# Gate and up products of a two-part fp32r matmul: one 512-column product takes the x parts side by side, their halves are added on the way out

## The chip, the cores and the metric

The kernel runs on one core of a Trainium2 chip. The metric is the device time of one execution in microseconds (us). TensorE (PE) multiplies, with weight loads on a row of their own (PEld); VectorE (DVE) and ScalarE (ACT) work beside it; GpSimd (POOL) has almost nothing to do; SyncE (SP) issues the DMAs.

## The reference

Two layers of: half-step SwiGLU, a hybrid mixer (sliding-window attention beside gated linear attention), half-step SwiGLU; 256 tokens, width 1024, feed-forward width 2816, all in float32. The change touches the feed-forward blocks, of which there are four:

```python
def swiglu(x, w_gate, w_up, w_down):
    a = jnp.einsum('bsd,df->bsf', x, w_gate)
    u = jnp.einsum('bsd,df->bsf', x, w_up)
    return jnp.einsum('bsf,fd->bsd', jax.nn.silu(a) * u, w_down)

for l in range(2):
    x = x + 0.5 * swiglu(rmsnorm(x, ffn1_norm[l]), ffn1_w_gate[l], ffn1_w_up[l], ffn1_w_down[l])
    x = x + hybrid_mixer(rmsnorm(x, mix_norm[l]), ...)
    x = x + 0.5 * swiglu(rmsnorm(x, ffn2_norm[l]), ffn2_w_gate[l], ffn2_w_up[l], ffn2_w_down[l])
```

## The kernel before

**Two-part arithmetic.** Each fp32 operand is split into a rounded fp32r part and the fp32r rest: weights into `whi` and `wlo`, activations into `xhi` and `xlo` (or `h_parts` for the hidden values). A product is then three matmuls into the same place in PSUM: whi with xhi, whi with xlo, wlo with xhi (`three`, lines 356 to 358). Tokens are the moving operand: 256 columns; the stationary operand is a 128x128 block of weights, loaded anew for each of the three.

**Units.** The weights come in units of 256 columns of gate or up weights (or 256 rows of down weights), 1 MB each, in three slots that go round: `raw` is filled by a DMA, ACT rounds it into `whi` (`split_hi`, line 791), DVE subtracts for `wlo` (`split_lo`, line 1021), and then PE may start. A gate or up unit has two tiles of 128 hidden features (`FT` = 2) and eight blocks of the contraction (`KT` = 8), so 16 triples; a down unit too. `unit_done` counts finished units; ACT waits on it before it overwrites a slot.

**A feed-forward block** has 11 groups of 256 hidden features. PE's order is: gate and up of group 0 (banks 2 and 7, at the end of the stage before), gate and up of group 1, down of group 0, and in a loop gate of g, up of g, down of g-1; at the end down of group 10 (`finish`). Gate products of groups 1 to 10 go to PSUM bank 0, up products to bank 1. DVE multiplies them on their way out by `rB`, the row of 1/rms values (`gate_out`, line 1103; `up_out`, line 1108), ACT takes the silu (line 816), DVE multiplies both (line 1111), ACT and DVE split the result (lines 823 and 1115), and `hlo_done` lets the down unit of that group go. Down products accumulate in banks 4 to 7.

**The norm's detour.** The 1/rms values are spread over the partitions by TensorE into bank 3 (`spread_r`, line 413), in the midst of or just after the gate unit of group 1, and DVE copies them to `rB` (`norm_b`, line 1095; semaphore `rb_done`). Group 0's gate values wait in bank 2 for that, and `a_done` counts gate values that have left.

Of the kernel before, what the change touches and what calls it, by code (L numbers as in the profile page):

```python
# [22 lines left out]
F32 = mybir.dt.float32  # L23
F32R = mybir.dt.float32r
I32 = mybir.dt.int32
ALU = mybir.AluOpType
# [69 lines left out]
def trunk(nc, xt, par_d, gain0_d, cst_d, fg, fu, fd, w_in, w_out, out):  # L96
    ctx = ExitStack()
    with ctx:
# [12 lines left out]
        xhi = sb("xhi", [P, KT, SEQ], F32R)  # L111
        xlo = sb("xlo", [P, KT, SEQ], F32R)
# [51 lines left out]
        sg = sb("sg", [P, 4, SEQ])  # L164
        at32 = work[:, 0:4, :]
# [6 lines left out]
        ps = [ctx.enter_context(nc.psum_tensor(f"ps{i}", [P, 512], F32)) for i in range(8)]  # L172
# [47 lines left out]
        rb_done = sem("rb_done")  # L220
        a_done, silu_done, u_done, h_done, hhi_done, hlo_done = (
# [132 lines left out]
        def _(pe):  # L354
# [19 lines left out]
            def up(slot, turn, bank):  # L374
                split_ready(slot, turn)
                for ft in range(FT):
                    last = up_tile(tiles(bank)[:, ft, :], slot, ft)
                last.then_inc(unit_done, 1)
# [58 lines left out]
            def first_pieces(u, bank):  # L437

                for p in range(PIECES):
                    if p < PIECES - 1:  # L440
                        pe.wait_ge(lo_piece, (PIECES - 1) * u + p + 1)
                    else:
                        split_ready(u, 0)
                    for ft in range(FT):
                        for k in (2 * p, 2 * p + 1):
                            w_hi, w_lo = weights(u, k, UC, ft * P, P)
# [53 lines left out]
            def ffn(f, l):  # L500
# [284 lines left out]
        def _(act):  # L785
# [27 lines left out]

            def silu(n):
# [10 lines left out]
            def ffn(f, l, after):  # L825
# [20 lines left out]
                split_hi(2, t + g)  # L846
                silu(grp + g)
                h_hi(1, grp + g)
# [167 lines left out]
        def _(dve):  # L1016
# [83 lines left out]
            def gate_out(n, unit, bank=0):  # L1100

                dve.wait_ge(unit_done, ST + unit + 1)
                nc.vector.tensor_tensor(a32[:, :, :], tiles(bank), r_tiles(2), ALU.mult).then_inc(a_done, 1)  # L1103

            def up_out(n, unit, bank=1):

                dve.wait_ge(unit_done, ST + unit + 1)
                nc.vector.tensor_tensor(u32[:, :, :], tiles(bank), r_tiles(2), ALU.mult).then_inc(u_done, 1)  # L1108
# [9 lines left out]
            def ffn(f, l, v, after):  # L1118
# [6 lines left out]
                gate_out(grp, 3 * t, 2)  # L1125
                up_out(grp, 3 * t + 1, 7)
                split_lo(1, t + 1)
                h_lo(0, grp)
                with dve.Fori(1, GROUPS - 1) as g:

                    split_lo(2, t + g)
                    gate_out(grp + g, 3 * (t + g) - 1)

                    split_lo(0, t + g + 1)
                    up_out(grp + g, 3 * (t + g))
# [5 lines left out]
                gate_out(grp + g, 3 * (t + g) - 1)  # L1141
                up_out(grp + g, 3 * (t + g))
# [328 lines left out]
```

## Time and profile before

| | |
|---|---|
| median of 3 runs | 964.71 us (963.52 to 965.16) |
| the profiled execution | 965.2 us, its span from first to last instruction 963.2 us |
| PE matmul, PE weight load | 950.4 us (99%), 942.7 us (98%) of the span |
| DVE, ACT | 613.3 us (64%), 456.5 us (47%) |
| mean granted TensorE clock | 0.993 |
| mean HBM traffic | 176 GB/s |

A busy PE is not a PE at its peak: matmuls are pipelined, so that a row's length (some 0.28 us) is more than twice the step from one row's start to the next. The steps are what counts, and they are read from the start times.

### The profile page before, as it was taken

To read this page: it belongs to the slowest core of one execution; us is meant where nothing else is said; L and a number is where in the kernel's file an instruction comes from. 1 tells how busy PE (TensorE), PEld (TensorE's weight loads), DVE (VectorE), ACT (ScalarE), POOL (GpSimd) and SP (SyncE) were. 2 spreads that over 40 slices of the span, in tenths; PEclk is the share of its full clock that TensorE was granted. 3 is DMA by queue.
4 is the path that set the end of the run, shared out by engine and by line. 5 is a ranking of instruction groups with operands and counts; after the bars stand their busy time and mean duration, and the time that the engine had idled before them with its cause. 6 is when DMAs were issued, how large, how long until landed. Compare 5 with 4: busy or idle time off the path is not lost.

```text
span 963.2 us, 19406 instructions
## 1 busy us (share of the span) xinstructions
PE 950.4 (99%) x8188; PEld 942.7 (98%) x8188; DVE 613.3 (64%) x732; ACT 456.5 (47%) x490; POOL 2.8 (0%) x6
## 2 busy tenths in 40 slices
PE   8999999999999999999999999999999999999996
PEld 8999999999999999999999999999999999999996
DVE  6756555587758665555686555557786785555653
ACT  6433443457645433443554344346584634334332
POOL 0000000000000000000000000000000000000001
PEclk9999999999999999999999999999999999999997
DMA  8665565553246665555556555555522665656621
GB/s 284 216 216 176 184 203 180 178 179 118 77 153 200 210 202 175 185 195 187 174 191 209 174 186 194 186 177 167 183 66 70 216 220 189 203 174 190 201 87 44
DMA packets 130613, 169.05 MB, mean 176 GB/s; under 512 B 3216, under 2 KB 116112, under 8 KB 130576
## 3 DMA queue, kind: packets, MB, share of 16 engines
q1 hardware_dynamic: 130576, 168.52, 54.4%
q8 instruction: 28, 0.46, 0.2%
q14 instruction: 9, 0.07, 0.0%
HBM read 167.46 MB, written 1.05 MB: 175 GB/s over the span
## 4 chain that ended last, share of the span: by engine, by line
PE 93%; DVE 3%; ACT 2%; DMA 1%; issue 0%; SPq 0%; POOL 0%; DVEq 0%
PE ps L356 29%; PE ps L357 29%; PE ps L358 29%; PE ps L413 1%; PE ps L563 1%; DMA raw<-in_ffn_w_gate 1%; PE ps L576 1%; DVE resid L1048 0%; DVE wlo L1021 0%; PE ps L722 0%; ACT sq L812 0%; ACT whi L791 0%; PE ps L700 0%; DVE work L1291 0%; DVE xlo L1026 0%
## 5 line engine op out<-in xcount | busy, mean ns | idle before, releaser
L1021 DVE TENSOR_TENSOR wlo<-raw,whi 128x2048 fp32r<-128x2048 f32 (+1 forms) x159 | 355.9, 2239 | 252.9 <-ACT whi L791 252.9
L356 PE MATMUL ps<-xhi,whi 128*128 128x256 f32 x1680 | 471.9, 281 | 0.0
L357 PE MATMUL ps<-xlo,whi 128*128 128x256 f32 x1680 | 470.7, 280 | 0.0
L358 PE MATMUL ps<-xhi,wlo 128*128 128x256 f32 x1680 | 469.3, 279 | 0.0
L791 ACT ACTIVATE whi<-raw 128x2048 fp32r<-128x2048 f32 (+1 forms) x159 | 297.3, 1870 | 166.1 <-PE ps L358 160.1
L356 PEld LDWEIGHTS ps<-xhi,whi 128*128 128x128 f32 x1680 | 316.2, 188 | 1.7 <-issue 1.0
L357 PEld LDWEIGHTS ps<-xlo,whi 128*128 128x128 f32 x1680 | 315.9, 188 | 0.0
L358 PEld LDWEIGHTS ps<-xhi,wlo 128*128 128x128 f32 x1680 | 315.0, 187 | 0.0
L356 PE MATMUL ps<-h_parts,whi 128*128 128x256 f32 x768 | 212.7, 277 | 0.0
L357 PE MATMUL ps<-h_parts,whi 128*128 128x256 f32 x768 | 212.4, 277 | 0.0
L358 PE MATMUL ps<-h_parts,wlo 128*128 128x256 f32 x768 | 212.3, 276 | 0.0
L356 PEld LDWEIGHTS ps<-h_parts,whi 128*128 128x128 f32 x768 | 144.4, 188 | 0.1
L358 PEld LDWEIGHTS ps<-h_parts,wlo 128*128 128x128 f32 x768 | 144.4, 188 | 0.0
L357 PEld LDWEIGHTS ps<-h_parts,whi 128*128 128x128 f32 x768 | 144.4, 188 | 0.0
L823 ACT ACTIVATE h_parts<-work 128x512 fp32r<-128x512 f32 x44 | 27.8, 633 | 145.0 <-DVE work L1111 145.0
L816 ACT ACTIVATE work<-work 128x512 f32<-128x512 f32 x44 | 27.8, 632 | 131.9 <-DVE work L1103 131.9
L1115 DVE TENSOR_TENSOR h_parts<-work,h_parts 128x512 fp32r<-128x512 f32 x44 | 30.5, 692 | 30.8 <-ACT h_parts L823 30.8
L1108 DVE TENSOR_TENSOR work<-ps,rB 128x512 f32<-128x512 f32 x44 | 30.1, 684 | 3.0 <-PE ps L358 3.0
L1111 DVE TENSOR_TENSOR work<-work 128x512 f32<-128x512 f32 x44 | 30.5, 693 | 2.1 <-ACT work L816 0.7
L1103 DVE TENSOR_TENSOR work<-ps,rB 128x512 f32<-128x512 f32 x44 | 30.2, 686 | 0.1
L1048 DVE SCALAR_TENSOR_TENSOR resid<-ps,resid 128x512 f32<-128x512 f32 x24 | 16.6, 690 | 11.2 <-PE ps L358 11.2
L805 ACT ACTIVATE xhi<-resid,par 128x256 fp32r<-128x256 f32 x40 | 18.2, 503 | 7.7 <-DVE resid L1048 7.3
(150 smaller groups left out, 485.5 us busy)
## 6 DMA issues: line engine op xcount, KB each, us to landing
raw<-in_ffn_w_down SPq DMA_DIRECT2D x44, 1024.0 KB, 4.9
raw<-in_ffn_w_up SPq DMA_DIRECT2D x43, 1024.0 KB, 5.3
raw<-in_ffn_w_gate SPq DMA_DIRECT2D x42, 1024.0 KB, 5.4
raw<-in_w_in SPq DMA_DIRECT2D x12, 1024.0 KB, 5.2
raw<-in_w_in SPq DMA_DIRECT2D x8, 512.0 KB, 4.6
raw<-in_w_out SPq DMA_DIRECT2D x8, 512.0 KB, 4.4
raw<-in_w_in SPq DMA_DIRECT2D x2, 1088.0 KB, 5.2
raw<-in_ffn_w_gate SPq DMA_DIRECT2D x8, 256.0 KB, 7.1
```

The costliest lines, as they stand in the source:

```text
L356: pe.matmul(o, w_hi, x_hi, start=start, stop=False, skip_group_check=True)
L357: pe.matmul(o, w_hi, x_lo, start=False, stop=False, skip_group_check=True)
L358: return pe.matmul(o, w_lo, x_hi, start=False, stop=stop, skip_group_check=True)
L791: nc.scalar.activation(h, r, ACT.Copy).then_inc(hi_done, 1)
L805: nc.scalar.activation(xhi[:, m, :], resid[:, m, :], ACT.Copy, scale=gain[:, m:m + 1]).then_inc(xhi_done, 1)
L816: nc.scalar.activation(s32[:, :, :], a32[:, :, :], ACT.Silu).then_inc(silu_done, 1)
L823: nc.scalar.activation(hhi[hb][:, :, :], h32[:, :, :], ACT.Copy).then_inc(hhi_done, 1)
L1021: nc.vector.tensor_tensor(lo, r, h.bitcast(F32), ALU.subtract).then_inc(lo_done, 1)
L1103: nc.vector.tensor_tensor(a32[:, :, :], tiles(bank), r_tiles(2), ALU.mult).then_inc(a_done, 1)
L1108: nc.vector.tensor_tensor(u32[:, :, :], tiles(bank), r_tiles(2), ALU.mult).then_inc(u_done, 1)
L1111: nc.vector.tensor_tensor(h32[:, :, :], s32[:, :, :], u32[:, :, :], ALU.mult).then_inc(h_done, 1)
L1115: nc.vector.tensor_tensor(hlo[hb][:, :, :], h32[:, :, :], hhi[hb][:, :, :].bitcast(F32), ALU.subtract).then_inc(hlo_done, 1)
```

## The change

`xhi` and `xlo` become two halves of one tensor `x_parts`, side by side for each contraction block, and the gate and up units of groups 1 to 10 of each feed-forward block use them as one moving operand of 512 columns: whi is loaded once for both, and the result goes to a whole bank, whi·xhi in its first half and whi·xlo in its second. The third product, wlo with xhi, has 256 columns and accumulates on the first half. A gate or up unit of two tiles so fills two banks, `gate_ps` (banks 0 and 1) and `up_ps` (banks 2 and 3). On the way out ACT copies the second halves to SBUF (`cross`, in the space of the mixer's `PT`), DVE adds the first halves to that, and a further DVE instruction multiplies by `rB`. Group 0, the down units and the mixer keep `three`. Since banks 2 and 3 hold group 0's gate values and the spread 1/rms values, PE waits for `rb_done` and `a_done` before the up unit of group 1.

```diff
-        xhi = sb("xhi", [P, KT, SEQ], F32R)
-        xlo = sb("xlo", [P, KT, SEQ], F32R)
+        x_parts = sb("x_parts", [P, KT, 2, SEQ], F32R)
+        xhi, xlo = x_parts[:, :, 0, :], x_parts[:, :, 1, :]
...
+        cross = PT[:, :, :].rearrange("p h c -> p (h c)")[:, 0:4 * SEQ].rearrange("p (u f t) -> p u f t", u=2, f=FT)
+
+        def wide_halves(wide):
+            parts = wide[:, :].rearrange("p (f a t) -> p f a t", f=FT, a=2)
+            return parts[:, :, 0, :], parts[:, :, 1, :]
...
-        ps = [ctx.enter_context(nc.psum_tensor(f"ps{i}", [P, 512], F32)) for i in range(8)]
+        gate_ps = ctx.enter_context(nc.psum_tensor("gate_ps", [P, 1024], F32))
+        up_ps = ctx.enter_context(nc.psum_tensor("up_ps", [P, 1024], F32))
+        ps = [w[:, 512 * i:512 * i + 512] for w in (gate_ps, up_ps) for i in range(2)]
+        ps += [ctx.enter_context(nc.psum_tensor(f"ps{i}", [P, 512], F32)) for i in range(4, 8)]
...
+            def wide_two(wide, slot, ft, k):
+
+                o = wide[:, 512 * ft:512 * ft + 512]
+                w_hi, w_lo = weights(slot, k, UC, ft * P, P)
+                pe.matmul(o, w_hi, x_parts[:, k, :, :].rearrange("p a t -> p (a t)"),
+                          start=k == 0, stop=False, skip_group_check=True)
+                return pe.matmul(o[:, 0:SEQ], w_lo, xhi[:, k, :], start=False, stop=k == KT - 1,
+                                 skip_group_check=True)
...
-                    up_tile(tiles(0)[:, 0, :], 2, 0)
+                    wide_tile(gate_ps, 2, 0)
                     spread_r(5 * l + 4 * f, rs_y)
-                    up_tile(tiles(0)[:, 1, :], 2, 1).then_inc(unit_done, 1)
-                up(0, t + 1, 1)
+                    wide_tile(gate_ps, 2, 1).then_inc(unit_done, 1)
+                pe.wait_ge(rb_done, v + 1)
+                pe.wait_ge(a_done, grp + 1)
+                up_wide(0, t + 1, up_ps)
                 pe.wait_ge(hlo_done, grp + 1)
...
                 with pe.Fori(2, GROUPS) as g:
                     pe.wait_ge(a_done, grp + g)
-                    up(2, t + g - 1, 0)
+                    up_wide(2, t + g - 1, gate_ps)
                     pe.wait_ge(u_done, grp + g)
-                    up(0, t + g, 1)
+                    up_wide(0, t + g, up_ps)
...
+            def cross_out(unit, u, wide):
+
+                act.wait_ge(unit_done, ST + unit + 1)
+                nc.scalar.copy(cross[:, u, :, :], wide_halves(wide)[1]).then_inc(cross_done, 1)
...
                 split_hi(2, t + g)
+                cross_out(3 * (t + g) - 1, 0, gate_ps)
                 silu(grp + g)
+                cross_out(3 * (t + g), 1, up_ps)
                 h_hi(1, grp + g)
...
+            def wide_out(i, u, wide, dst, done):
+
+                dve.wait_ge(cross_done, 2 * i + u + 1)
+                nc.vector.tensor_tensor(dst[:, :, :], cross[:, u, :, :], wide_halves(wide)[0], ALU.add
+                                        ).then_inc(wide_step, 1)
+                dve.wait_ge(wide_step, 2 * i + u + 1)
+                nc.vector.tensor_tensor(dst[:, :, :], dst[:, :, :], r_tiles(2), ALU.mult).then_inc(done, 1)
```

On PE, at the first up unit of the first feed-forward block (`L413` or `L438` is `spread_r`, what follows is the up unit of group 1), the order before is:

```order
L358 MATMUL ps<-xhi,wlo 128x256
L413 MATMUL ps<-cst,rs_y 128x128 [waits rs_step]
L413 MATMUL ps<-cst,rs_y 128x128
L356 MATMUL ps<-xhi,whi 128x256 [waits lo_done]
L357 MATMUL ps<-xlo,whi 128x256
L358 MATMUL ps<-xhi,wlo 128x256
```

and now:

```order
L390 MATMUL gate_ps<-x_parts,wlo 128x256
L438 MATMUL up_ps<-cst,rs_y 128x128 [waits rs_step]
L438 MATMUL up_ps<-cst,rs_y 128x128
L388 MATMUL up_ps<-x_parts,whi 128x512 [waits lo_done,a_done,rb_done]
L390 MATMUL up_ps<-x_parts,wlo 128x256
L388 MATMUL up_ps<-x_parts,whi 128x512
```

A triple has become a pair, and the up unit's first matmul waits for DVE twice more.

On ACT, the end of a feed-forward block (last gate and up group, after the loop; `L791` or `L821` is `split_hi`, `L816` or `L851` the silu, `L823` or `L858` is `h_hi`) before:

```order
L791 ACTIVATE whi<-raw 128x2048 [waits unit_done,loaded2]
L816 ACTIVATE work<-work 128x512 [waits a_done]
L823 ACTIVATE h_parts<-work 128x512 [waits h_done]
L791 ACTIVATE whi<-raw 128x2048 [waits unit_done,loaded0]
L791 ACTIVATE whi<-raw 128x2176 [waits unit_done,loaded1]
```

and now:

```order
L821 ACTIVATE whi<-raw 128x2048 [waits unit_done,loaded2]
L847 COPY PT<-gate_ps 128x512 [waits unit_done]
L851 ACTIVATE work<-work 128x512 [waits a_done]
L847 COPY PT<-up_ps 128x512 [waits unit_done]
L858 ACTIVATE h_parts<-work 128x512 [waits h_done]
L821 ACTIVATE whi<-raw 128x2048 [waits unit_done,loaded0]
```

Two copies out of PSUM have come in, the second one behind the silu.

On DVE, the same place (`L1021` or `L1060` is `split_lo`, `L1111` or `L1155` the product of silu and up, `L1115` or `L1159` is `h_lo`) before:

```order
L1021 TENSOR_TENSOR wlo<-raw,whi 128x2048 [waits hi_done]
L1103 TENSOR_TENSOR work<-ps,rB 128x512 [waits unit_done]
L1108 TENSOR_TENSOR work<-ps,rB 128x512 [waits unit_done]
L1111 TENSOR_TENSOR work<-work 128x512 [waits silu_done,u_done]
L1115 TENSOR_TENSOR h_parts<-work,h_parts 128x512 [waits hhi_done]
```

and now:

```order
L1060 TENSOR_TENSOR wlo<-raw,whi 128x2048 [waits hi_done]
L1147 TENSOR_TENSOR work<-PT,gate_ps 128x512 [waits cross_done]
L1150 TENSOR_TENSOR work<-work,rB 128x512 [waits wide_step]
L1147 TENSOR_TENSOR work<-PT,up_ps 128x512 [waits cross_done]
L1150 TENSOR_TENSOR work<-work,rB 128x512 [waits wide_step]
L1155 TENSOR_TENSOR work<-work 128x512 [waits silu_done,u_done]
L1159 TENSOR_TENSOR h_parts<-work,h_parts 128x512 [waits hhi_done]
```

Each value that leaves PSUM now takes two DVE instructions, and waits for ACT's copy instead of for PE.

## Rows read from the trace of the kernel before

**Rows 1.** The page: busy time, share of the span and instructions of each engine

```profile
PE 950.4 (99%) x8188; PEld 942.7 (98%) x8188; DVE 613.3 (64%) x732; ACT 456.5 (47%) x490; POOL 2.8 (0%) x6
```

**Rows 2.** The page: the chain that ended last, share of the span

```profile
PE 93%; DVE 3%; ACT 2%; DMA 1%; issue 0%; SPq 0%; POOL 0%; DVEq 0%
```

**Rows 3.** Timeline of PE, one loop turn: start us, length us, engine, line, operation

```profile
157.92 0.28 PE L356 MATMUL ps<-xhi,whi 128*128 128x256 f32 x1
...
169.23 0.28 PE L356 MATMUL ps<-h_parts,whi 128*128 128x256 f32 x1
...
174.68 0.28 PE L356 MATMUL ps<-xhi,whi 128*128 128x256 f32 x1
```

**Rows 4.** Timeline of PE, mixer of layer 1, where the clock is halved

```profile
738.28 0.42 PE L358 MATMUL ps<-xhi,wlo 128*128 128x256 f32 x1
...
740.42 0.41 PE L356 MATMUL ps<-h_parts,whi 128*128 128x256 f32 x1
```

**Rows 5.** Windows: busy us of PE, PEld, DVE, ACT, POOL; clock, DMA share, GB/s

```profile
738.30:740.30 2.00, 2.00 (x11) 2.00 (x11) 0.54 (x4) 0.00 (x0) 0.00 (x0) 0.50 0.00 0
157.90:169.20 11.30, 11.30 (x98) 11.30 (x97) 6.24 (x5) 4.90 (x4) 0.00 (x0) 1.00 0.57 188
```

**Rows 6.** Timeline of PE, mixer of layer 0: products with one moving column

```profile
266.12 1.92 PE L722 MATMUL ps<-ones,sq 128*128 128x1 f32 x16 [0.27 <-ACT sq L948]
```

**Rows 7.** Timeline of PE, mixer of layer 0: 272 moving columns, the widest there are

```profile
206.38 0.29 PE L356 MATMUL ps<-whi,xhi 128*128 128x272 f32 x1
...
208.90 0.29 PE L358 MATMUL ps<-whi,xlo 128*128 128x272 f32 x1
```

**Rows 8.** Timeline of PE and of DVE, group 1 of the first feed-forward block

```profile
28.99 0.60 PE L413 MATMUL ps<-cst,rs_y 128*128 128x128 f32 x4
29.35 0.36 PE L356 MATMUL ps<-xhi,whi 128*128 128x256 f32 x1
...
30.09 0.69 DVE L1103 TENSOR_TENSOR work<-ps,rB 128x512 f32<-128x512 f32 x1
```

**Rows 9.** Timeline of PE and of DVE, group 1 of the second block

```profile
312.75 0.28 PE L358 MATMUL ps<-xhi,wlo 128*128 128x256 f32 x1
...
310.69 0.69 DVE L1103 TENSOR_TENSOR work<-ps,rB 128x512 f32<-128x512 f32 x1
```

**Rows 10.** Groups of instructions by line and shape: busy us, mean ns, idle before

```profile
L946 ACT COPY work<-ps 128x512 f32<-128x512 f32 x4 | 2.3, 568 | 0.0
...
L1111 DVE TENSOR_TENSOR work<-work 128x512 f32<-128x512 f32 x44 | 30.5, 693 | 2.1 <-ACT work L816 0.7
L1103 DVE TENSOR_TENSOR work<-ps,rB 128x512 f32<-128x512 f32 x44 | 30.2, 686 | 0.1
```

**Rows 11.** Timelines of DVE, ACT and PE, last group of the first block

```profile
182.54 2.29 DVE L1021 TENSOR_TENSOR wlo<-raw,whi 128x2048 fp32r<-128x2048 f32 x1 [2.65 <-ACT whi L791]
184.75 0.68 DVE L1103 TENSOR_TENSOR work<-ps,rB 128x512 f32<-128x512 f32 x1
...
188.30 0.69 DVE L1115 TENSOR_TENSOR h_parts<-work,h_parts 128x512 fp32r<-128x512 f32 x1 [0.70 <-ACT h_parts L823]
...
185.47 0.63 ACT L816 ACTIVATE work<-work 128x512 f32<-128x512 f32 x1 [2.96 <-DVE work L1103]
187.63 0.63 ACT L823 ACTIVATE h_parts<-work 128x512 fp32r<-128x512 f32 x1 [1.54 <-DVE work L1111]
...
180.33 0.28 PE L356 MATMUL ps<-xhi,whi 128*128 128x256 f32 x1
...
185.98 0.28 PE L356 MATMUL ps<-h_parts,whi 128*128 128x256 f32 x1
...
191.43 0.28 PE L356 MATMUL ps<-h_parts,whi 128*128 128x256 f32 x1
```

**Rows 12.** Timelines of ACT and DVE in the loop turn of rows 3

```profile
163.78 1.91 ACT L791 ACTIVATE whi<-raw 128x2048 fp32r<-128x2048 f32 x1 [2.97 <-PE ps L358]
...
167.93 0.69 DVE L1103 TENSOR_TENSOR work<-ps,rB 128x512 f32<-128x512 f32 x1
```

More of the change, by code:

```diff
@@ L220, in trunk @@
         rb_done = sem("rb_done")
+        cross_done, wide_step = sem("cross_done"), sem("wide_step")
         a_done, silu_done, u_done, h_done, hhi_done, hlo_done = (
@@ L372, in up_tile, with wide_tile, up_wide @@
                 return last
-            def up(slot, turn, bank):
+            def wide_two(wide, slot, ft, k):
[5 more added lines that the diff above has]
+                                 skip_group_check=True)
+            def wide_tile(wide, slot, ft):
+                for k in range(KT):
+                    last = wide_two(wide, slot, ft, k)
+                return last
+            def up_wide(slot, turn, wide):
                 split_ready(slot, turn)
                 for ft in range(FT):
-                    last = up_tile(tiles(bank)[:, ft, :], slot, ft)
+                    last = wide_tile(wide, slot, ft)
                 last.then_inc(unit_done, 1)
@@ L445, in first_pieces @@
                         for k in (2 * p, 2 * p + 1):
+                            if u == 2:
+                                last = wide_two(gate_ps, u, ft, k)
+                                continue
                             w_hi, w_lo = weights(u, k, UC, ft * P, P)
@@ L846, in ffn @@
                 split_hi(2, t + g)
+                cross_out(3 * (t + g) - 1, 0, gate_ps)
                 silu(grp + g)
+                cross_out(3 * (t + g), 1, up_ps)
                 h_hi(1, grp + g)
@@ L1098, in r_tiles, with first_out, h_out @@
                 return rB[:, :].unsqueeze(1).to_broadcast([P, n, SEQ])
-            def gate_out(n, unit, bank=0):
+            def first_out(unit, bank, dst, done):
                 dve.wait_ge(unit_done, ST + unit + 1)
[L1103 to L1108, printed above, removed]
+                nc.vector.tensor_tensor(dst[:, :, :], tiles(bank), r_tiles(2), ALU.mult).then_inc(done, 1)
+            def wide_out(i, u, wide, dst, done):
[4 more added lines that the diff above has]
+                nc.vector.tensor_tensor(dst[:, :, :], dst[:, :, :], r_tiles(2), ALU.mult).then_inc(done, 1)
+            def h_out(n):
                 dve.wait_ge(u_done, n + 1)
@@ L1124, in ffn @@
                 dve.wait_ge(rb_done, v + 1)
-                gate_out(grp, 3 * t, 2)
-                up_out(grp, 3 * t + 1, 7)
+                first_out(3 * t, 2, a32, a_done)
+                first_out(3 * t + 1, 7, u32, u_done)
+                h_out(grp)
                 split_lo(1, t + 1)
                 h_lo(0, grp)
+                wide0 = (2 * l + f) * (GROUPS - 1) - 1
                 with dve.Fori(1, GROUPS - 1) as g:
                     split_lo(2, t + g)
-                    gate_out(grp + g, 3 * (t + g) - 1)
+                    wide_out(wide0 + g, 0, gate_ps, a32, a_done)
                     split_lo(0, t + g + 1)
-                    up_out(grp + g, 3 * (t + g))
+                    wide_out(wide0 + g, 1, up_ps, u32, u_done)
+                    h_out(grp + g)
                     h_lo(0, grp + g)
@@ L1140, in ffn @@
                 split_lo(2, t + g)
-                gate_out(grp + g, 3 * (t + g) - 1)
-                up_out(grp + g, 3 * (t + g))
+                wide_out(wide0 + g, 0, gate_ps, a32, a_done)
+                wide_out(wide0 + g, 1, up_ps, u32, u_done)
+                h_out(grp + g)
                 h_lo(1, grp + g)
```

## Prediction

> **What bounds the kernel now.** I read the page first: PE's matmul row is busy 99% of the span and its weight-load row 98%, while DVE has 64% and ACT 47% [rows 1]. The chain of work that ended last is PE for 93% of the span [rows 2]. So time is won or lost in how fast PE steps from one matmul to the next, and the other engines matter only where PE comes to wait for them. The timeline gives the step. In one loop turn the gate unit and the up unit take 96 matmuls from 157.92 to 169.23 us, and the down unit 48 matmuls from there to 174.68 [rows 3]: 11.31 / 96 = 117.8 ns and 5.45 / 48 = 113.5 ns each, in both cases 256 moving columns over a 128x128 block of weights. No gap is to be seen between units. A triple of the gate and up units is 3 x 117.8 = 353.4 ns.
>
> What is in a step of 117.8 ns? In layer 1's mixer there is a stretch with the clock granted at 0.50 [rows 5], which is 1.2 instead of 2.4 GHz, and there ten matmuls of 256 columns take 738.28 to 740.42 [rows 4], 214 ns each. Half of that, 107 ns, is the streaming of 256 columns at full clock. The full-clock step is 10.8 ns longer. A matmul with one moving column, whose streaming is nothing, steps at (1.92 - 0.25) / 15 = 111 ns [rows 6] (0.25 being what the last row's length adds, an estimate from the 0.28 of the other rows): that is what loading 128 columns of weights costs. So at 256 columns the stream (107) and the load beneath it (111) are nearly the same length, and the step lies a little above both. At half clock the stream of 214 ns hides the load wholly, and nothing is left over it.
>
> **The change, part by part.** It touches 4 blocks x 20 units (gate and up, groups 1 to 10) x 16 triples = 1280 triples. Each loses one matmul and one weight load, and becomes one matmul of 512 columns and one of 256.
>
> *The 512-column step.* No row has 512 columns. From below: 214 ns, the half-clock row, where a stream of equal length stands over a load of the same size. From above, by the widest row there is: 20 steps of 272 columns take 206.38 to 208.90 [rows 7], 126 ns each or 0.463 ns per column, and at that rate 512 columns take 237 ns. Between them lies a fixed extra of 10.8 ns, as 256 columns have it: 225 ns. I take 217, near the lower end, since the half-clock row is nearest in what matters: a load with twice its own time to hide in.
>
> *The 256-column step behind it.* Under it the load for the next wide product has to go, as now; I keep 117.8. The lower end is the load alone, 111.
>
> *Sum on PE.* 217 + 117.8 = 334.8 ns against 353.4: 18.6 ns less, times 1280 = 23.8 us less. The ends: 214 + 111 = 325 gives 36.4 us less; 225 + 117.8 = 342.8 gives 13.6 us less; 237 + 117.8 = 354.8 gives 1.8 us more.
>
> Here a rule speaks against the change. The row shows 117.8 ns where the stream is 107. By the Trainium skill ("TensorE: Matmul & The Clock Gate", section "Back-to-back issue gap"), a warm matmul's gap is its columns over 2.4 plus about 2.5 ns, so that a triple would be 327.5 now and 325 after: a saving of 2.5 ns per triple, 3.2 us in all, in place of my 23.8. The trace disagrees with the first of these figures by 26 ns per triple. The same section also gives a sustained 131 ns per pair of load and matmul at 512 columns. With it a pair would be 249 ns and the gain 134 us; no row here streams faster than 256 columns in 113.5 ns, which is 227 ns for 512.
>
> *The way out.* Per gate or up unit ACT gets a copy of 512 elements out of PSUM, 0.57 us, and DVE one more instruction of 0.69 [rows 10]: 80 x 0.57 = 46 us on ACT and 80 x 0.69 = 55 us on DVE. Both have room: in a gate and up stretch of 11.3 us DVE is busy 6.24 and ACT 4.90 [rows 5]. What counts is lateness. In the loop, gate values leave at 167.93 to 168.62 [rows 12]; now `a_done` comes some 0.75 later, and after it, in ACT's order, the silu, the next `split_hi`, the copy of the up halves. I follow it from the end of a gate unit, T = 157.92 + 48 x 0.1178 = 163.57, with the durations of these rows (`split_hi` 1.91, `split_lo` 2.29, the small steps 0.57 to 0.69 [rows 10, 11, 12]): the gate value begins to leave at T+4.4 and is done at T+5.8, silu T+6.5, `split_hi` T+8.4, copy T+9.0, `split_lo` T+10.7, up value T+12.1, h T+12.8, its two parts T+14.2, and the next `split_hi` and `split_lo` at T+17.7. PE wants h's parts and that slot at T+21.5 (an up, a down, a gate and an up unit later), and the next turn begins for ACT at T+16.2, when it is free. So nothing is late, and the work costs nothing while 3.8 us of cover remain.
>
> *The last group* has no such cover. PE starts its down unit (`finish`) straight after down of group 9, at 191.43, and the last part of h is ready at 188.30 + 0.69 = 188.99 [rows 11]. Now, from `split_lo`'s end at 184.75 on: add and multiply to 186.16, silu to 186.82, copy to 187.4, add and multiply to 188.83, product to 189.55, high part to 190.21, low part to 190.94. PE begins that group's up unit at 180.33 and so arrives at 180.33 + 16 x 0.3348 + 48 x 0.1135 = 191.14. A margin of 0.2 us where there were 2.4; if the pair is 325 ns, 0.04. I put 0.2 us for all four blocks together, and up to 1 us if an added step is 0.25 us longer than its row.
>
> *The new wait ahead of group 1's up unit.* In the first block PE spreads 1/rms at 28.99, begins the up unit at 29.35, and group 0's gate values leave bank 2 only at 30.09 + 0.69 = 30.78 [rows 8]. The wait stops PE for 30.78 - 29.35 plus some 0.1 to start again: 1.5 us. All later weights are queued behind it on PE, nothing else. In the three other blocks the spread is issued in the middle of the gate unit: the bank is free at 310.69 + 0.69 = 311.38, PE gets there at 312.75 [rows 9], or 0.15 sooner with faster pairs. No wait; the cover is 1.2 us.
>
> **Sum.** 965.2 (the profiled execution) - 23.8 + 1.5 + 0.2 = 943.1 us. The median before is 0.5 lower, 964.71, so 943 us, 2.3% less.
>
> **The rivals.**
>
> *The extra is a fixed price per matmul.* Then 225 + 117.8, and 965.2 - 13.6 + 1.7 - 0.5 = 952.8 us. For it: 272 columns also have more than their stream (126 against 114). Against it: the half-clock row, where the extra is nil. Chance 0.22.
>
> *The 256-column step gets shorter too*, towards the load's 111, because its own weights are ready long before: 325 ns, 965.2 - 36.4 + 1.7 - 0.5 = 930 us; half-way is 937. Chance of a step clearly shorter than I take, so that the time is below 936: 0.07.
>
> *The time goes with columns.* If the moving operand is read at 117.8 / 256 = 0.46 ns per column, 512 take 235.6, a pair is 353.4, nothing is saved, and the waits are left: 966 us. The fixed part alone could be small: 3 ns less per triple is 3.8 us, 962.6 us or, with the waits, about 963. The skill's formula, above, is of this kind. Measured, all these are no change. Chance 0.09. The 131 ns figure, by which the time would be about 831 us, gets 0.01.
>
> *Slower: a wide product steps at the rate of the 272-column row or worse.* 237 + 117.8 = 354.8 ns, 1.8 us more, and with the waits 965.2 + 1.8 + 1.7 - 0.5 = 968 us. From 256 to 272 columns the step grows by (126 - 117.8) / 16 = 0.5 ns per column, more than the stream's 0.42, which speaks for it; at 0.5 on all further columns 512 take 249 and the time is 984. Against it: the half-clock stretch has no such slope. It decides from 237 ns for 512 columns on. Chance 0.09.
>
> **How the numbers follow.** My forecast, roughly 936 to 948 us, has 0.52; the fixed price, 948 to 956, has 0.22; the shorter step 0.07; no gain 0.09; slower 0.09; the last 0.01 is far below all of them. Faster is the sum of the first three and the last. A measurement of this kernel tells some 0.2% (2 us) from no change. Faster 0.82, same 0.09, slower 0.09. The range 933 to 958 leaves out the two cases without a gain and the shortest times.
>
> **What would show it.** In the timeline of PE a loop turn's gate and up units: 32 pairs in about 10.7 us against 11.31, with starts 217 and 118 ns apart; down units unchanged at 5.45. In the waits of PE a new one of about 1.3 to 1.5 us at the first wide up unit, for DVE's work tile, and none at the three others. At each `finish` a gap under 0.1 us. DVE at some 668 us busy, ACT at 502. The prediction is wrong if the wide step is over 230 ns, if the last group's chain is longer than its rows say, or if the first wait is followed by a stretch at half clock, which would cost up to 1.7 us (3.4 us at half speed, as in layer 1's mixer).

## The result and the profile after

The changed kernel takes 971.56 us (median of 5 runs, 969.62 to 972.06) against 965.16 us of the kernel before beside it (5 runs, 963.52 to 967.22): a ratio of 1.0058, 95% interval 1.0041 to 1.0074. It is slower by 0.6%, and the forecast of 943 us was wrong in size and in sign. The profiled execution took 969.62 us, its span 967.7 us, at a mean clock of 0.996.

The page of the changed kernel, busy time of each engine and its costliest PE groups, answers to [rows 1]:

```profile
PE 954.3 (99%) x6908; PEld 888.4 (92%) x6908; DVE 668.2 (69%) x812; ACT 489.5 (51%) x570; POOL 2.8 (0%) x6
...
L388 PE MATMUL up_ps<-x_parts,whi 128*128 128x512 f32 x640 | 227.9, 396 | 1.3 <-DVE rB L1134 1.3
L388 PE MATMUL gate_ps<-x_parts,whi 128*128 128x512 f32 x640 | 228.0, 396 | 0.0
```

1280 matmuls and 1280 weight loads are gone (8188 to 6908), and PE is busy for 3.9 us longer. DVE has the forecast's 668 us. PE's matmul row says only that it never rests; the steps have to be read from start times, as before.

The timeline of PE, changed kernel, two loop turns (`L388` is the wide product, `L390` the one of wlo, `L366` the first of a down unit):

```profile
142.94 0.40 PE L388 MATMUL gate_ps<-x_parts,whi 128*128 128x512 f32 x1
143.18 0.28 PE L390 MATMUL gate_ps<-x_parts,wlo 128*128 128x256 f32 x1
...
154.26 0.28 PE L366 MATMUL ps<-h_parts,whi 128*128 128x256 f32 x1
...
159.91 0.39 PE L388 MATMUL gate_ps<-x_parts,whi 128*128 128x512 f32 x1
160.14 0.28 PE L390 MATMUL gate_ps<-x_parts,wlo 128*128 128x256 f32 x1
160.25 0.39 PE L388 MATMUL gate_ps<-x_parts,whi 128*128 128x512 f32 x1
160.48 0.28 PE L390 MATMUL gate_ps<-x_parts,wlo 128*128 128x256 f32 x1
160.60 0.40 PE L388 MATMUL gate_ps<-x_parts,whi 128*128 128x512 f32 x1
160.83 0.28 PE L390 MATMUL gate_ps<-x_parts,wlo 128*128 128x256 f32 x1
...
171.20 0.28 PE L366 MATMUL ps<-h_parts,whi 128*128 128x256 f32 x1
...
176.64 0.40 PE L388 MATMUL gate_ps<-x_parts,whi 128*128 128x512 f32 x1
```

Three things stand here. First, a wide step takes 0.23 us, then one of 0.12 follows; over all pairs of the loops the means are 233.4 and 119.7 ns, 353.1 together. The 32 pairs of a turn take 11.29 and 11.32 us by turns, where the 96 matmuls of [rows 3] took 11.31. **The pair costs what the triple cost.** Second, the down unit, which the change doesn't touch, takes 159.91 - 154.26 = 5.65 us in one turn and 176.64 - 171.20 = 5.44 us in the next: 117.7 and 113.3 ns per matmul. This alternates from turn to turn; only the last two down units of a block, which follow each other with no pair between them, are of the same kind. 21 of the 44 down units of the feed-forward blocks are of the slow kind, where before all 44 had 113.3. Third, the waits of PE:

```profile
PE up_ps L438 <- DVE rs_y L1113: 2.4, 1, 2.4
PE up_ps L388 <- DVE rB L1134: 1.3, 1, 1.3
PE up_ps L438 <- DVE rcol L1113: 1.3, 2, 0.8
```

The one of `L388` is new, 1.3 us, once, in the first block, as forecast. The view names `rB`, but DVE's copy to it ended at 29.84; PE starts again at 30.67, 0.1 us after group 0's gate values have left the bank (29.88 + 0.69), so it is the wait for them that ends last. At the last group nothing waits: in the first block the low part of h is ready at 192.14 + 0.69 = 192.83, and PE needs it at 193.61; in the second, where the last down units are of the fast kind, 0.57 us are left as well (477.67 against 478.24).

The sum in the profiled executions: pairs 0, slow down units 21 x 48 x 4.44 ns = 4.5 us, wait 1.3 us, together 5.8 where the spans differ by 4.5. Before's profiled execution had the half-clock stretch of [rows 4], worth up to 1.7 us, and the changed one, at PE clock 1.00 there, had none. Profiles at equal clock, below, remove this.

### The profile page after: what moved, and what is told of

It reads as the page before. It is cut to its first block, busy times and chain, and to the rows that moved or that the text cites. A ratio compares the mean times of both kernels' runs of the same rounds, so it can differ in the third digit from the quotient of the medians.

```text
span 967.7 us, 17046 instructions
## 1 busy us (share of the span) xinstructions
PE 954.3 (99%) x6908; PEld 888.4 (92%) x6908; DVE 668.2 (69%) x812; ACT 489.5 (51%) x570; POOL 2.8 (0%) x6
## 4 chain that ended last, share of the span: by engine, by line
PE 90%; DVE 4%; ACT 3%; issue 1%; DMA 1%; SPq 0%; POOL 0%; DVEq 0%; ACTq 0%
PE gate_ps L388 15%; PE up_ps L388 15%; PE ps L366 10%; PE ps L368 10%; PE ps L367 10%; PE gate_ps L390 8%; PE up_ps L390 8%; PE gate_ps L366 2%; PE gate_ps L368 2%; PE gate_ps L367 2%; DVE wlo L1060 1%; ACT whi L821 1%; PE up_ps L366 1%; PE up_ps L367 1%; PE up_ps L368 1%
## 5 line engine op out<-in xcount | busy, mean ns | idle before, releaser
L1060 DVE TENSOR_TENSOR wlo<-raw,whi 128x2048 fp32r<-128x2048 f32 (+1 forms) x159 | 355.9, 2239 | 206.0 <-ACT whi L821 206.0
L821 ACT ACTIVATE whi<-raw 128x2048 fp32r<-128x2048 f32 (+1 forms) x159 | 296.3, 1866 | 115.4 <-PE gate_ps L390 64.5
L388 PE MATMUL up_ps<-x_parts,whi 128*128 128x512 f32 x640 | 227.9, 396 | 1.3 <-DVE rB L1134 1.3
L388 PE MATMUL gate_ps<-x_parts,whi 128*128 128x512 f32 x640 | 228.0, 396 | 0.0
L366 PE MATMUL ps<-h_parts,whi 128*128 128x256 f32 x768 | 214.0, 279 | 0.0
L390 PE MATMUL up_ps<-x_parts,wlo 128*128 128x256 f32 x640 | 180.4, 282 | 0.0
L390 PE MATMUL gate_ps<-x_parts,wlo 128*128 128x256 f32 x640 | 180.4, 282 | 0.0
L388 PEld LDWEIGHTS up_ps<-x_parts,whi 128*128 128x128 f32 x640 | 120.3, 188 | 30.6 <-DVE rB L1134 1.5
L366 PEld LDWEIGHTS ps<-h_parts,whi 128*128 128x128 f32 x768 | 144.2, 188 | 1.8
L388 PEld LDWEIGHTS gate_ps<-x_parts,whi 128*128 128x128 f32 x640 | 120.3, 188 | 26.9
L390 PEld LDWEIGHTS gate_ps<-x_parts,wlo 128*128 128x128 f32 x640 | 120.3, 188 | 0.0
L390 PEld LDWEIGHTS up_ps<-x_parts,wlo 128*128 128x128 f32 x640 | 120.2, 188 | 0.0
L858 ACT ACTIVATE h_parts<-work 128x512 fp32r<-128x512 f32 x44 | 27.8, 632 | 156.8 <-DVE work L1155 156.8
L851 ACT ACTIVATE work<-work 128x512 f32<-128x512 f32 x44 | 27.8, 633 | 142.2 <-DVE work L1150 129.8
L1150 DVE TENSOR_TENSOR work<-work,rB 128x512 f32<-128x512 f32 x80 | 55.4, 693 | 2.8
L1159 DVE TENSOR_TENSOR h_parts<-work,h_parts 128x512 fp32r<-128x512 f32 x44 | 30.4, 691 | 30.7 <-ACT h_parts L858 30.7
L366 PE MATMUL gate_ps<-x_parts,whi 128*128 128x256 f32 x160 | 46.0, 287 | 0.0
L366 PE MATMUL ps<-x_parts,whi 128*128 128x256 f32 x160 | 45.3, 283 | 0.0
```

The source lines that it names most:

```text
L366: pe.matmul(o, w_hi, x_hi, start=start, stop=False, skip_group_check=True)
L388: pe.matmul(o, w_hi, x_parts[:, k, :, :].rearrange("p a t -> p (a t)"), start=k == 0, stop=False, skip_group_check=True)
L390: return pe.matmul(o[:, 0:SEQ], w_lo, xhi[:, k, :], start=False, stop=k == KT - 1, skip_group_check=True)
L821: nc.scalar.activation(h, r, ACT.Copy).then_inc(hi_done, 1)
L851: nc.scalar.activation(s32[:, :, :], a32[:, :, :], ACT.Silu).then_inc(silu_done, 1)
L858: nc.scalar.activation(hhi[hb][:, :, :], h32[:, :, :], ACT.Copy).then_inc(hhi_done, 1)
```

## The experiments

Two theories stood against each other. **By column:** a step is columns times some 0.46 ns, however many matmuls and loads they are cut into. **By load:** the 10.8 ns that 256 columns have above their stream come from the weight load beneath, and are less under a wide product. What came to matter most, where the data stand in SBUF, came up as a rival in the first batch.

### Is it the columns, the loads, or the width?

**a_nolo**: the changed kernel without the product of wlo in the 1280 pairs.

```diff
-                pe.matmul(o, w_hi, x_parts[...], start=k == 0, stop=False, ...)
-                return pe.matmul(o[:, 0:SEQ], w_lo, xhi[:, k, :], start=False, stop=k == KT - 1, ...)
+                last = pe.matmul(o, w_hi, x_parts[...], start=k == 0, stop=k == KT - 1, ...)
```

> The changed kernel without the wlo products of the wide units (1280 matmuls of 256 columns left out, so the result is less exact): 512-column matmuls follow each other. If the time goes with columns: the step stays at 234 to 236 ns. If there is a fixed extra per matmul of 10.8 ns over the stream: 224. If the 233.7 of the changed kernel is the price of the short matmul beside it: 214 to 217. PE may then wait for the other engines between units, which says nothing on the step.

One execution: 913.89 us. Timeline of PE, 14 wide products in a row, and the down unit behind them:

```profile
135.37 3.38 PE L388 MATMUL up_ps<-x_parts,whi 128*128 128x512 f32 x14
140.33 0.38 PE L366 MATMUL ps<-h_parts,whi 128*128 128x256 f32 x1 [1.58 <-DVE wlo L1059]
```

3.38 us less the last one's length of 0.39 over 13 steps is 230 ns, each with one load of 128 columns beneath it. That is more than twice 113.3, and not 214 to 217: giving the load double its time doesn't take the extra away, though it is 3 ns less here than beside the short matmul. (The time itself says little, since PE now waits for DVE, 1.58 us in most turns.)

**a_256**: the changed kernel with the wide product taken apart again; all waits, banks, copies and additions stay.

```diff
-                pe.matmul(o, w_hi, x_parts[...], start=k == 0, stop=False, ...)
+                pe.matmul(o[:, 0:SEQ], w_hi, xhi[:, k, :], start=k == 0, stop=False, ...)
+                pe.matmul(o[:, SEQ:2 * SEQ], w_hi, xlo[:, k, :], start=False, stop=k == KT - 1, ...)
```

> The changed kernel with the wide product taken apart again: whi with xhi into the bank's first half, whi with xlo into its second, 256 columns each, everything else (banks, copies, added halves, the waits) as changed. If time goes with columns, joining two products is worth nothing: three steps of 117.8 ns, and the time is that of the changed kernel but for what the down units' steps do (113.4 or 117.8, 4.5 us between half and none of them slow), 967 to 972. If the joined product did save something and the way out ate it: 10 us or more above the changed kernel, 982 or more.

970.81 us, ratio 1.0043 to before (1.0013 to 1.0072), within the changed kernel's interval. The steps of x are 117.8 ns. At this placement, joining two products into one is worth nothing, and so are 1280 loads fewer. The down units are slow here too, but in whole blocks (the first and the third), not in every second turn: the alternation comes with the wide shape, the slow kind doesn't need it.

### The places of the operands

Each placement is made with unused tensors ahead of and behind the one that is moved, for example:

```diff
+        pad_a = sb("pad_a", [P, 32])
         xhi = sb("xhi", [P, KT, SEQ], F32R)
         xlo = sb("xlo", [P, KT, SEQ], F32R)
+        pad_b = sb("pad_b", [P, 32])
```

A pad of 16 columns is 64 bytes, 32 are 128, 80 are 320. In the kernel before, within 256 bytes, the weights start at 128, x's parts at 192 and h's at 64. I call the address of the moving operand less that of the weights, modulo 256, its distance: 64 for x, 192 for h. No trace lists addresses; the distances follow from the order and the sizes of the tensors, if each begins at a multiple of 32 bytes.

> The kernel before with 64 bytes of padding ahead of xhi and 192 behind xlo, so that only the place of the x parts moves (from 192 to 0 modulo 256 bytes); all tensors behind move by 256. Theory A, the extra of 4.4 ns per step in gate and up units over down units comes from where the moving operand starts: the step falls from 117.8 to 113.4 ns, 5040 steps of this kind gain some 20 us. Theory B, it comes from something else (order of the blocks, the data, a phase carried over): step 117.8, time within 2 us of before.

> The changed kernel with the same padding around x_parts. If the place of the moving operand sets the rate (A): the 512-column step falls from 233.7 towards 227, twice 113.4, the pair from 353.5 towards 340, and the time by some 17 us and 4 more in the down units. If not (B): pair 353.5, time within 2 us of the changed kernel.

> The kernel before with 128 bytes of padding ahead of xhi, so that the x parts start at 64 modulo 256 bytes as h_parts does. Under A with the start modulo 256 as the cause: step 113.4. Under B: 117.8.

> The changed kernel with x_parts moved by 128 bytes, to 64 modulo 256 as h_parts. In the kernel before the same shift let gate and up units step at 113.4 in one block and 117.8 in the others, always the same as the down units. If the pair follows: 227 + 113 = 340 ns in units of the fast kind, 353.5 in those of the slow kind, one kind over whole blocks; time between 951 (all fast) and 976 (all slow).

> The kernel before with h_parts moved instead, to 192 modulo 256 as xhi and xlo. If it is equal places modulo 256 that let x and h units share their kind (as with x moved to 64): gate and up units at 113.4 in some blocks. If 192 itself is a slow place: all steps, down units too, at 117.8, 10 us more than before.

The next ones put all at a multiple of 256 bytes (b_al before, a_al changed), x alone at one of 1024 (b_x320), and two more distances (b_s1, b_s3).

> The kernel before with paddings ahead of raw, xhi and h_parts, so that raw and wlo, xhi, xlo and h_parts start at a multiple of 1024 bytes and whi at 512 modulo 1024. If the places of weights and moving operand relative to each other or to a wide line cost the extra over the 107 ns stream, every step falls to 113.4 or less: 20 us less than before, or 40 if it falls to 109. If 0 modulo 256 is what x64 tried (steps of 115 to 122 in gate and up units) whatever the rest: 10 us more than before.

> The changed kernel with the same places. If all steps go at 113.4 per 256 columns: pairs of 340 ns, 947 us. If the extra has nothing to do with places: 967 to 976 us.

> The kernel before with only xhi and xlo moved, to 0 modulo 1024. Set beside x64 (0 modulo 256, 768 modulo 1024): the same steps (115 to 122, mean 119) if only the place modulo 256 counts, others if 1024 does.

> The kernel before with xhi and xlo at 224 and h_parts at 160 bytes, both counted modulo 256 from where whi and wlo start. So far: distance 0 gives 120 ns (all tensors on one line), 64 gives 117.8 (before: x), 128 gives 115 to 122 (x64), 192 gives 113.4 or 117.8 (h_parts in before, both in x128). Theory R, this distance between the moving operand and the weights being loaded beneath it sets the step: 224 and 160 give steps of their own kind, one for each, between 107 and 120. Rival: the places of the single tensors count, or nothing regular: steps of several kinds in one stretch.

> The kernel before with xhi and xlo at 32 and h_parts at 96 bytes modulo 256 from the start of the weights. Theory R: two further kinds of steps; by the neighbours (0: 120, 64: 117.8, 128: mean 118.6) both lie at 117 to 120 ns, and the time is 10 to 20 us above before. If only the distance 192 has a fast kind by chance of a restart, nothing here is at 113.4.

What was measured, steps in ns by differences of start times in the loops, times in us, the median with the ratio to before and its interval where there are several executions, else one execution (before had medians of 965.2 to 967.0 beside them):

| kernel | x, h distance | x step (or wide, next) | h step | time |
|---|---|---|---|---|
| before | 64, 192 | 117.8 | 113.3 | 965.16 |
| b_h128 | 64, 64 | 117.8 | 117.8 | 972.08 |
| b_x64 | 128, 192 | 118.7 (115 to 122) | 113.3 or 117.8 by block | 977.93, 1.0123 (1.0094 to 1.0152) |
| b_x320 | 128, 192 | as b_x64 | as b_x64 | 976.93 |
| b_x128 | 192, 192 | 113.3 in block 1, then 117.8 | the same | 966.05 |
| b_s1 | 224, 160 | 118.3 | 117.3 to 118.7 | 977.23 |
| b_s3 | 32, 96 | 117.8 or 117.9, in block 2 116.7 | 119.8 to 120.0 | 977.93 |
| b_al | 0, 0 | 120.0 | 120.0 | 989.23, 1.0235 (1.0188 to 1.0282) |
| changed | 64, 192 | 233.4, 119.7 | 113.3, 117.8 in turn | 971.56, 1.0058 (1.0041 to 1.0074) |
| a_x64 | 128, 192 | 230.7, 120.0 | 117.8, the first of each block near 113.6 | 974.04, 1.0068 (1.0045 to 1.0091) |
| a_x128 | 192, 192 | 235.0, 118.3 | 117.8 | 973.25, 1.0073 (1.0056 to 1.009) |
| a_al | 0, 0 | 236.4, 117.1 | 120.0 | 982.48, 1.0174 (1.0123 to 1.0224) |

Several of these were expected otherwise. b_x64 was to gain 20 us or nothing and lost 11; b_al was to gain 20 us or more, or lose 10, and lost 23; a_al was to take 947 us or 967 to 976 and took 982; the pair of a_x64 was to take 340 or 353.5 ns and took 350.7. That the places matter came out; which place is good did not follow from any theory here.

The timeline of PE in b_al, first product of a down unit, of the next gate unit and of the next down unit:

```profile
155.82 0.28 PE L359 MATMUL ps<-h_parts,whi 128*128 128x256 f32 x1
...
161.58 0.28 PE L359 MATMUL ps<-xhi,whi 128*128 128x256 f32 x1
...
173.10 0.28 PE L359 MATMUL ps<-h_parts,whi 128*128 128x256 f32 x1
```

5.76 / 48 and 11.52 / 96 are both 120.0 ns, with the same instructions in the same order as [rows 3]: the program alone doesn't set the step, the addresses do. That b_x320 equals b_x64 speaks for 256 bytes as the period. x's parts stand at 0 in b_x64 (118.7) and in b_al (120.0), so that x's own place alone doesn't set its step; that leaves the weights' place, which differs between the two, and the distance. The weights were moved in b_al and a_al alone, all other distances were made by moving x and h: that the distance sets the step fits every row, but wasn't tried with other weights' places. Among the triples, the step at distance 64 was 117.8 in every kernel, whether the operand was x or h. Only at 192 did any unit have a mean near 113.3, and there not always.

Traffic of the DMAs is not what sets the 117.8. In layer 0's mixer of the kernel before, 168 matmuls with x's parts step on evenly at 117.8 ns, from 283.70 to 303.49 us, while the DMA share falls from 1.01 to 0.17 (the columns are those of [rows 5]):

```profile
290.00:296.00 6.00, 6.00 (x53) 6.00 (x53) 5.28 (x10) 4.33 (x8) 0.00 (x0) 1.00 1.01 336
296.00:302.00 6.00, 6.00 (x53) 6.00 (x53) 5.07 (x7) 5.71 (x7) 0.00 (x0) 1.00 0.17 35
```

The wide shape has its own dependence. At distance 0 a triple is 3 x 120.0 = 360.0 and the pair 353.5, and there the change does bring something: 1280 x 6.5 ns = 8.3 us, less the wait of 1.3, where a_al was 6.8 us faster than b_al on the same chip. At 128 it is 356.0 against 350.7: 6.8 us, less the wait and 7 more slow down units (40 against 33, 1.5 us), makes 4.0, where a_x64 was 3.9 us faster than b_x64. At 64, where the kernel stands, it is nil, and at 192 the pair has the slow kind's 353.4 where the triple may have 340.

Three of the means are 106.7 ns, the stream, plus multiples of 6.67: one (113.3), two (120.0), five per three matmuls (117.8). Those of b_x64, b_s1 and b_s3 don't fall into this so simply, and no run shows what a unit of 6.67 ns would be. At half clock there was nothing above the stream [rows 4].

### The wait, and the alternation

**a_early**: the changed kernel with the first block's `spread_r` issued in the middle of the gate unit.

```diff
                 for p in range(PIECES):
+                    if u == 2 and p == 2:
+                        spread_r(0, rs_y)
...
-                    spread_r(0, rs_y)
```

> The changed kernel with the first block's spread of 1/rms issued in the middle of the gate unit, as in the other blocks, in place of behind it. The wait ahead of the first wide up unit, 1.3 us, falls to 0.3 or less. Time 1 us less than the changed kernel if nothing else moves; if the kind of the down units (113.4 or 117.8 ns) is set by the phase at a restart, it may come out differently in whole blocks, by up to 5 us either way.

969.36 us, 1.0034 (1.0013 to 1.0054). The waits of PE:

```profile
PE up_ps L491 <- ACT whi L828: 2.6, 3, 1.1
PE up_ps L438 <- DVE rs_y L1114: 2.4, 1, 2.4
```

The wait at the up unit is gone, and 2.6 us of waits for the pieces of the first weights are listed instead of 0.5. The intervals of this one and of the changed kernel overlap, so what it won can't be told from nothing: its median is 2.2 us lower, but its profiled span, 968.4 us with 21 slow down units, is only 0.5 us under that of the changed kernel profiled again below, with 22. The alternation stays.

**a_break**: the changed kernel with a product of one zero column (it adds nothing to the result) ahead of each down unit but a block's first, 40 in all.

```diff
+                if not first:
+                    pe.matmul(acc[0][:, 0, 0:1], ones[:, :], zcol[:, 0:1], start=False, stop=False, ...)
```

> The changed kernel with one product of a single column of zeros ahead of each down unit but the first of a block (40 in all). Theory P, a phase carried over from the unit before sets whether a down unit steps at 113.4 or 117.8 ns: the strict alternation of fast and slow down units ends; all alike, fast if the restart favours it (minus 4.5 us for 21 units, plus 40 times 0.2 for the product). Rival D, the data or the buffers of each group set it: the alternation stays as it is.

981.02 us in one execution. The alternation is gone: all 40 down units with the product ahead are slow, 117.8 ns, and of the four without it those of blocks 1 and 3 are fast. So the kind is no property of a down unit's data; what PE did just before it decides, by a state that no view shows, and one more small product shifts it. That this product would reset it to the fast kind was wrong.

The wide pairs have kinds too. Two stretches of 32 pairs in this trace, from the first `L389` to the zero product `L409` behind the up unit:

```profile
77.04 0.39 PE L389 MATMUL gate_ps<-x_parts,whi 128*128 128x512 f32 x1
...
88.33 0.28 PE L409 MATMUL ps<-zcol,ones 128*128 128x1 f32 x2
...
94.20 0.40 PE L389 MATMUL gate_ps<-x_parts,whi 128*128 128x512 f32 x1
...
105.37 0.28 PE L409 MATMUL ps<-zcol,ones 128*128 128x1 f32 x2
```

11.29 / 32 is 352.8 ns a pair, 11.17 / 32 is 349.1, and so on by turns: at the same distance of 64 the pair isn't bound to 353 either.

### Is the kind set anew?

Both kernels were profiled again, and the placement with x and h at distance 192 was timed.

> The kernel before, unchanged, profiled again on another chip. If the kind of the h steps (113.3 or 117.8 ns) follows from the program and its addresses, all 44 down units of the loop are at 113.3 ns again and the time is 965 +- 1 us. If it is decided anew in each execution, some blocks' down units are at 117.8, 2.4 us per block more.

> The changed kernel, unchanged, profiled again. If its alternation of down units between 113.3 and 117.8 ns follows from the program, it stands here again with 21 of 44 slow and 970 to 972 us. If it is decided anew in each execution, the pattern is another one and the span moves with it by 0.21 us per down unit.

> The kernel before with the x parts moved 128 bytes on, timed: it is the one placement in which x and h steps could both take 113.3 ns, 4.3 us less per block in which they do. If the kind is the same as in the one look (first block alone fast), the ratio is 1.000 +- 0.002; if it changes between executions, the times spread over several us, the lowest some 950 us.

b_same: 965.09 us, span 963.1; all 44 down units at 113.3 again. a_same: 970.88 us, span 968.9 at the same clock of 0.994. The alternation is there again, but started with the other kind in the third block, so that 22 down units are slow: 22 x 48 x 4.44 ns = 4.7 us, with the wait of 1.3 makes 6.0, and the spans differ by 5.8. This closes the sum to 0.2 us. The alternation comes again with the program, its start doesn't.

b_x128t: median 965.47 us, but from 952.28 to 968.1 over 12 executions, three times at 952 to 953, twice at 959 to 960, seven times at 965 to 968. Before had 965.96 beside it, so by the medians it is the same; the recorded ratio, 0.9945 (0.991 to 0.998), is without the three longest, 966.96 to 968.1, and flatters it. The profiled one took 952.68. Its timeline of PE, a loop turn in the first block and one in the last:

```profile
149.62 0.28 PE L358 MATMUL ps<-h_parts,whi 128*128 128x256 f32 x1
...
155.06 0.28 PE L358 MATMUL ps<-xhi,whi 128*128 128x256 f32 x1
...
165.94 0.28 PE L358 MATMUL ps<-h_parts,whi 128*128 128x256 f32 x1
...
807.98 0.28 PE L358 MATMUL ps<-h_parts,whi 128*128 128x256 f32 x1
...
824.94 0.28 PE L358 MATMUL ps<-h_parts,whi 128*128 128x256 f32 x1
```

A turn of 144 matmuls takes 16.32 us in the first block (113.3 each) and 16.96 in the last (117.8), the same code at the same addresses. In this execution three blocks are of the fast kind, in the single one of b_x128 (966.05) one was: 13.4 us for two blocks. 11 turns x 0.64 = 7.0 us per block gives 14, and would explain the steps between the three groups of times. So at distance 192, with triples alone, the kind is set for each block anew and kept through its loop.

The mixers show where the kind can change. The kernel before, with its 44 fast down units, has the slow kind there: timeline of PE, layer 0's mixer, 48 matmuls with `h_parts`, the spread of 1/rms, and 48 more with `h_parts` up to `L356` with `xhi`:

```profile
270.81 0.28 PE L356 MATMUL ps<-h_parts,whi 128*128 128x256 f32 x1
...
276.46 1.95 PE L413 MATMUL ps<-cst,rs_y 128*128 128x128 f32 x16
278.17 0.37 PE L356 MATMUL ps<-h_parts,whi 128*128 128x256 f32 x1
...
283.70 0.28 PE L356 MATMUL ps<-xhi,whi 128*128 128x256 f32 x1
```

The first 48 take 5.65 us, 117.7 each; the second 5.53, of which the first step takes 0.20 and the others 113.4. Layer 1's mixer and the repetition b_same have the same. So something between two units can change the kind within 2 us. A stop of PE alone needn't: in a_nolo PE stops ahead of all 44 down units, mostly for 1.6 us, and 39 of them are fast. What does it was not tried by itself.

**b_swap**: the mirror image. x's and h's parts both 128 bytes on, so that x has distance 192 and h 64.

```diff
+        pad_a = sb("pad_a", [P, 32])
         xhi = ...
         xlo = ...
+        pad_b = sb("pad_b", [P, 32])
...
+        pad_c = sb("pad_c", [P, 32])
         h_parts = ...
+        pad_d = sb("pad_d", [P, 32])
```

> The kernel before with x parts and h parts both moved 128 bytes on, so that the x steps now have the distance to the weights that the h steps had (192 modulo 256 bytes), and the h steps that of the x steps (64). If the fast kind follows the distance, and a stretch at distance 64 ahead of it always leads into the fast kind, as in the kernel before: h steps 117.8, x steps of a loop turn 113.3, 0.21 us less per turn, 956 us or a little less in every execution. If the kind at distance 192 is drawn at a restart alone, the x steps are at 113.3 in some blocks and at 117.8 in others, and the times spread from some 956 to 975. If it stays whatever precedes it, 974 us.

959.74 us (957.52 to 967.2, 12 executions), ratio 0.9938 (0.9911 to 0.9966). Timeline of PE, profiled execution, a turn in the first block and one in the second:

```profile
154.17 0.28 PE L360 MATMUL ps<-h_parts,whi 128*128 128x256 f32 x1
...
159.83 0.28 PE L360 MATMUL ps<-xhi,whi 128*128 128x256 f32 x1
...
171.13 0.28 PE L360 MATMUL ps<-h_parts,whi 128*128 128x256 f32 x1
...
319.54 0.28 PE L360 MATMUL ps<-h_parts,whi 128*128 128x256 f32 x1
...
325.19 0.28 PE L360 MATMUL ps<-xhi,whi 128*128 128x256 f32 x1
...
336.08 0.28 PE L360 MATMUL ps<-h_parts,whi 128*128 128x256 f32 x1
```

h takes 117.8 ns everywhere (5.66 / 48). The 96 steps of x take 11.30 us in the first block, 117.7 each, and 10.89 in the second, 113.4; the third and fourth are like the second. The fast kind has gone over to x with the distance. It is again set by block, so that units at distance 64 ahead of it don't force it; the expected 956 us in every execution was wrong. This is the fastest version by its ratio, though its interval overlaps that of b_x128t: unused bytes alone, none of the change, 0.6% under the kernel before.

## Why the prediction was wrong

**"The 512-column step."** This is the step that failed: "I take 217, near the lower end, since the half-clock row is nearest in what matters: a load with twice its own time to hide in." It measured 233.4, over the 230 that the prediction had named as its sign of being wrong. All of the 23.8 us rest on it. The reasoning took stream (107) and load (111) as two rivals for the same 117.8 ns. But in a_nolo the load had its double time and the step was 230, and in b_al the same loads over the same columns took 120.0. The extra goes roughly with the columns (20 ns above the stream for 512, 11 for 256), with a price that depends on where the operands stand. Nor does the half-clock row show a hidden load: the load had double its time in a_nolo too, and 17 ns stayed. The row has the same width at another clock, and says nothing of a wider product at full clock. The 272-column row [rows 7], which I took for the far end, was near: 0.463 ns per column, 237 ns.

**"I keep 117.8"** for the step behind: near, 119.7.

**The rivals.** "The time goes with columns" was the one that came true, its 353.4 per pair against 353.1; it had 0.09. It gave 966 us, with the waits alone. "The extra is a fixed price per matmul" (225 ns) fell with the 233.4 itself and with a_nolo, 230 where it asked for 224; a_256 confirms that three matmuls take what the two do. Three of the rivals' figures are a microsecond or so off (half-way is 936, not 937; 131 ns gives 832, not 831; 3 ns less per triple is 961.4 without the waits), which moves no chance. The rule of the Trainium skill ("TensorE: Matmul & The Clock Gate", section "Back-to-back issue gap") would have 216 ns for 512 columns; no run here shows it, the lowest mean being 230 in a_nolo and the lowest single step 224 in a_x64. Its figure of 131 ns isn't seen either.

**"Down units unchanged at 5.45."** The second failure, and the one that gives the sign: half of them took 5.65, 4.5 to 4.7 us together. No step of mine asked whether the same instruction could have two speeds, though the trace of before had both, 113.5 for h and 117.8 for x in [rows 3], and I took this as a fact of the units. The mixer of the same trace had 117.7 and 113.4 for `h_parts` itself, as shown above.

**"The new wait"**: 1.5 forecast, 1.3 measured. **"The way out"** costs nothing: DVE 668.2 as said, ACT's copies have 0.565 us each as forecast, 45.2 in all, while its busy total rose by 33.0 only, to 489.5 against 502. The lengths of ACT's rows do add up to 44.4 us more, but rows in succession overlap, and busy time counts an overlap once; a copy starts 0.10 us before the row ahead of it ends:

```profile
165.75 1.92 ACT L821 ACTIVATE whi<-raw 128x2048 fp32r<-128x2048 f32 x1 [1.99 <-PE gate_ps L390]
167.57 0.56 ACT L847 COPY PT<-gate_ps 128x512 f32<-128x512 f32 x1
```

**"The last group"**: 0.2 us forecast, none seen, because nothing upstream of it became faster; the pairs, no quicker than triples, left it 0.78 us of cover in the first block and 0.57 in the second.

So 965.2 + 0 + 1.3 + 4.5 = 971.0, where the median is 971.56.

**What stays open.** Which part of the chip makes the extra. Why the kind at distance 192 was the fast one in all 8 blocks of two profiles of the kernel before, and in a_256 in only two of four; the change leaves the distances as they were. Whether the distance or the two places by themselves set the step. Some of before's executions beside the experiments, not profiled, took 970 to 973 us, which several blocks with slow down units would give, but no trace shows it. And a placement or a start that has the fast kind every time was not found: with both operands at 192 and all four blocks fast, one more step of 7 us down from 952.7 would lead to some 946 us, an estimate from the groups of b_x128t.

## What to carry to other kernels

Before a forecast of what fewer or wider matmuls bring, divide steps by columns at two widths of full-clock rows; where ns per column agree, as 0.460 and 0.463 did, merging products may bring nothing, as here, and what it needs for its results is lost; at two other placements of the same kernel it brought 4 and 7 us. A row at another clock is no stand-in for one at another width. If steps of the same shape differ in one trace, find what differs, since moving data by 64 or 128 bytes may be worth more than the change at hand; and time such a version over many executions, because one profile shows only one of its outcomes.

## What the runs showed of the hardware

- A 256-column fp32r matmul with its weight load took 113.3 to 120.0 ns at full clock with the places of the operands modulo 256 bytes, 965 us or 989 us for the whole kernel with the same instructions. The worst was b_al, distance 0 with all operands at multiples of 256 bytes.
- At distance 192 it took 113.3 or 117.8 ns. In kernels of triples alone this was the same through a block of some 150 us, and could be another in the next block or execution: 952 to 968 us for one and the same program. Beside the wide product at distance 64 it changed from one loop turn to the next.
- A 512-column product with half the loads per column took 230 to 236 ns in the mean, and with its neighbour of 256 columns 353.1 to 353.5 ns at distances 0, 64 and 192 (350.7 at 128, and 349.1 in every second turn of a_break).
